# Recurrent scan: the triangular inversion on 32x32 diagonal blocks for its first four levels, joined to 64x64 in the fifth

## The chip, the cores and the metric

One Trainium2 chip, one of its cores. The metric is the device time of one execution, in microseconds. The kernel before takes 2808.89 us, the median of 3 runs (2808.25 to 2810.07).

## The reference, cut to what matters

The whole computation is two transformer blocks over 256 tokens (feed-forward layers, a differential attention, a recurrent mixer, memory and dilated attention). The change lies in the recurrent mixer alone, whose core is a scan over tokens, for each of 12 heads with a 64x64 state:

```python
def step(state, inp):
    r_t, w_t, k_t, v_t, kk_t, a_t = inp
    sa = jnp.einsum('bhvk,bhk->bhv', state, -kk_t)
    state = (state * w_t[:, :, None, :]
             + sa[..., None] * (kk_t * a_t)[:, :, None, :]
             + v_t[..., None] * k_t[:, :, None, :])
    return state, jnp.einsum('bhvk,bhk->bhv', state, r_t)
```

The term `sa` makes each token's update depend on the ones before it. Over a chunk of 64 tokens this is a system of equations with a unit lower triangular 64x64 matrix, so the scan can be done a chunk at a time once this matrix is inverted.

## The kernel before, in words

All of it runs on one core in float32. 97% of the span is TensorE work, most of it the products with the streamed weights (lines 2299 to 2301). The recurrent scan is a stretch of about 105 us without weight products, from 1909 to 2014 us of the span.

**Tiling of the scan.** The 12 heads are taken two at a time (RT = 6 iterations). A pair of heads has 4 chunks of 64 tokens for each head, so 8 triangular matrices of 64x64. They lie as 128 partitions (two chunks, rows `R[0]` and `R[1]`) by 4 units `m` of 64 columns. TensorE multiplies them as 64x64 tiles of its array, chunk 0 in rows and columns 0 to 63 and chunk 1 in 64 to 127. Each float32 matmul stands in the trace as two records.

**The inversion.** It grows the inverse `ti`, and its transpose `tit`, from blocks of 2 to 4, 8, 16, 32 and 64 in five levels. Level l of iteration i has four steps, each waiting for the one before:
- `level_p` (PE, L3017): P = L times `ti`, 8 matmuls into PSUM `INV[0]`
- `mask_p` (VectorE, L1982): the part of P that joins the blocks, into `pp`
- `level_t` (PE, L3030 and L3032): 8 matmuls for the growth of `ti` (not at level 4) and 8 for that of `tit`, into `INV[1]` and `INV[2]`
- `grow` (VectorE, L1988 and L1990): adds both to `ti` and `tit`

The matrices that it starts from come from `pairs_ti` (PE, L3000), `start_inverse` (VectorE, L1976 and L1978) and `start_transposed` (L1969 and L1970).

**The order.** It is written out by hand, for each engine, in a Python loop over i from 0 to 6. Between the steps of iteration i stand pieces of the neighbours: for i-1 the solution (`solve`, L3042), the read-out (`read_out`, L3055 to L3074), the state (`carry`, L3085) and the output (L3094); for i+1 the decay sums (L2939), the turn to token-major (L2968), the pairwise products (`pairs`, L2975), `pairs_ti` and `mix_values` (L3007). PE's order in a middle iteration is P0, solve, T0, decay sums, P1, read-out, T1, to tokens, P2, carry 0, pairs, T2, carry 1, pairs, P3, output, pairs, T3, pairs, P4, `pairs_ti`, T4, `mix_values`, where P and T are `level_p` and `level_t`. VectorE's queue has the same pieces in its own fixed order. ScalarE copies results out of PSUM (L1221 to L1242). Iteration 0 also carries the end of the weight splitting (L1315, 2.28 us each) and the bonus product (L2026) on VectorE.

Of the kernel before, what the change touches and what calls it, by code (L numbers as in the profile page):

```python
# [18 lines left out]
SHIFT = 8  # L19
# [8 lines left out]
CH = 64  # L28
# [25 lines left out]
def constants():  # L54

    p = np.arange(128)
    half = p // 64
    same = half[:, None] == half[None, :]
    parts = {}
    parts["ident"] = np.eye(128)  # L60
    parts["ones"] = np.ones((128, 128))
    parts["blk"] = same.astype(float)
    perm = np.zeros((128, 128))
    for f in range(128):
        perm[f ^ 16, f] = 1.0
# [24 lines left out]
    parts["lp_mask"] = np.concatenate([c_ < n_, c_ <= n_], 1).astype(float)  # L90
    def level(b, row, col):
        return ((row // (2 * b) == col // (2 * b)) & (row // b % 2 == 1) & (col // b % 2 == 0)).astype(float)
    parts["m1"], parts["m1t"] = level(1, c_, n_), level(1, n_, c_)
    for b in (2, 4, 8, 16, 32):
        parts[f"m{b}"] = level(b, c_, n_)


    parts["sel"] = np.zeros((128, 32))
    parts["sel"][p, 16 + half] = 1.0
    parts["sel8"] = np.zeros((128, 47))  # L100
    parts["sel8"][:, 39] = 1.0
    parts["spread"] = np.zeros((128, 8, 128))
    for i in range(8):
        parts["spread"][2 * i + half, i, p] = 1.0
        parts["spread"][32 + i, i] = 1.0
    parts["spread"] = parts["spread"].reshape(128, 1024)
    parts["ident64"] = np.concatenate([np.eye(64), np.eye(64)], 0)
# [167 lines left out]
def build(nc, W, ADA, AW, CB, XT, MEMT, VEC, CST, PM, BT, REL, LAM, W0B, LORA, GUP, OUT, stop=None):  # L275
# [13 lines left out]
    with ExitStack() as ctx:  # L289
# [154 lines left out]
              cst[:, cat["cos"]:cat["cos"] + 512].rearrange("p (m e n) -> p m e n", m=4, e=2)]  # L444
        xs = [cut(scr, 1024 + 1024 * j, 512, "p (m n) -> p m n", m=4) for j in range(2)]
        tx = cut(scr, 1536, 512, "p (m n) -> p m n", m=4)
        ti = cut(big, 7680 + SHIFT, 256, "p (m n) -> p m n", m=4)
        tit = [cut(hid, 0, 256, "p (m n) -> p m n", m=4), cut(scr, 8212, 256, "p (m n) -> p m n", m=4)]
        pp = cut(hid, 512, 256, "p (m n) -> p m n", m=4)
        ar = [cut(t, at, 512, "p (u e n) -> p u e n", u=2, e=2) for t, at in ((hid, 1024), (scr, 2560))]  # L450
        ends = cols[:, 24:36].rearrange("p (j c) -> p j c", j=3)

        VAR = [BANK[0], BANK[3]]
        MEAN = [BANK[i % 2][:, NX * (i // 2):NX * (i // 2 + 1)] for i in range(4)] + [BANK[2].rearrange("p (i n) -> p i n", n=NX)]
        Y_SQ = [lower[:, 8:10, :], lower[:, 10:12, :], hid[:, 1024:1536].rearrange("p (i n) -> p i n", n=NX)]
        INV = [ps_o[:, 0, 0:256], ps_o[:, 1, 0:256], ps_o[:, 1, 256:512]]
        FREE = [ps_o[:, 3, :], ps_g[:, 0, :], ps_u[:, 0, :], ps_u[:, 1, :], ps_g[:, 1, :]]
        be = cut(hid, 1536, 256, "p (u n) -> p u n", u=2)
        ka = cut(hid, 1792, 256, "p (u n) -> p u n", u=2)
# [841 lines left out]
        def _(dve):  # L1301
# [663 lines left out]

            def start_transposed(i):

                dve.wait_ge(rw["lpm"], 2 * i + 2)
                link(tt_(tit[i % 2], lp[i % 2][:, :, 0, :], over(C("m1t", CH), 4), mult))  # L1969
                tt_(tit[i % 2], tit[i % 2], over(C("ident64", CH), 4), add).then_inc(rw["tit"], 1)  # L1970

            def start_inverse(i):

                dve.wait_ge(rw["tib"], i + 1)
                for q, bank in enumerate((FREE[1], FREE[3])):
                    ins = tt_(ti[:, 2 * q:2 * q + 2, :], bank[:, 0:128].rearrange(by_unit, m=2), over(C("m1", CH), 2), mult)  # L1976
                link(ins)
                tt_(ti, ti, over(C("ident64", CH), 4), add).then_inc(rw["lmask"], 1)  # L1978

            def mask_p(i, l):  # L1980
                dve.wait_ge(rw["p"], 5 * i + l + 1)
                tt_(pp, INV[0].rearrange(by_unit, m=4), over(C(f"m{2 << l}", CH), 4), mult).then_inc(rw["pm"], 1)  # L1982

            def grow(i, l):

                dve.wait_ge(rw["t"], 5 * i + l + 1)
                if l < 4:
                    tt_(ti, ti, INV[1].rearrange(by_unit, m=4), add).then_inc(rw["ti"], 1)  # L1988
                t = tit[i % 2]
                tt_(t, t, INV[2].rearrange(by_unit, m=4), add).then_inc(rw["tt"], 1)  # L1990

            def readout(i):
                dve.wait_ge(rw["rp"], i + 1)
# [73 lines left out]
                pairs(0, q, "lp", lp, FREE[q], "lpm")  # L2067
            for q, b in enumerate((4, 0)):
                pairs(0, q, "mp", mp, FREE[b], "mpm")
            start_transposed(0)  # L2070
            start_inverse(0)
            for i in range(RT + 1):
                inv, post, pre = i < RT, i > 0, i + 1 < RT
                if inv:
# [209 lines left out]
        def _(pe):  # L2284
# [659 lines left out]
            for t in range(2, len(A_IN)):  # L2944
# [12 lines left out]
            R = [slice(0, 64), slice(64, 128)]  # L2957
            def tok(i, e, m):
                return tmaj[i % 2][:, e, m % 2, 64 * (m // 2):64 * (m // 2) + 64]

# [31 lines left out]
            def pairs_ti(i):  # L2992
                pe.wait_ge(rw["lpm"], 2 * i + 2)
                if i >= 2:
                    pe.wait_ge(rw["ss2"], 2 * (i - 1))
                for q in range(2):
                    for u in range(2):
                        for c in range(2):
                            t = slice(CH * c, CH * (c + 1))
                            ins = mm(FREE[1 + 2 * q][R[c], CH * u:CH * (u + 1)], ar[i % 2][R[q], u, 0, t], be[R[q], u, t], start=True, stop=True)  # L3000
                ins.then_inc(rw["tib"], 1)

            def mix_values(i):
# [6 lines left out]
            def level_p(i, l):  # L3010
                if l:
                    pe.wait_ge(rw["ti"], 4 * i + l)
                else:
                    pe.wait_ge(rw["lmask"], i + 1)
                for m in range(4):
                    for c in range(2):
                        ins = mm(INV[0][R[c], CH * m:CH * (m + 1)], lp[i % 2][R[c], m, 0, :], ti[R[c], m, :], start=True, stop=True)  # L3017
                ins.then_inc(rw["p"], 1)

            def level_t(i, l):  # L3020
                pe.wait_ge(rw["pm"], 5 * i + l + 1)
# [2 lines left out]
                else:  # L3024
                    pe.wait_ge(rw["tit"], i + 1)
                for m in range(4):
                    t = slice(CH * m, CH * (m + 1))
                    if l < 4:
                        for c in range(2):
                            mm(INV[1][R[c], t], tit[i % 2][R[c], m, :], pp[R[c], m, :], start=True, stop=True)  # L3030
                    for c in range(2):
                        ins = mm(INV[2][R[c], t], pp[R[c], m, :], tit[i % 2][R[c], m, :], start=True, stop=True)  # L3032
                ins.then_inc(rw["t"], 1)

            def solve(i):
# [224 lines left out]
```

## Time and profile before

| | |
|---|---|
| time, median of 3 | 2808.89 us |
| time of the profiled execution | 2802.01 us |
| its span | 2800.3 us |
| PE busy | 2706.9 us, 97% |
| VectorE (DVE) busy | 2045.4 us, 73% |
| ScalarE (ACT) busy | 1012.2 us, 36% |
| mean granted TensorE clock | 0.984 |

PE's busy time counts a matmul from its start to its modelled end, so it includes the latency after the last column. A stretch in which PE is called busy can still be one in which it waits for columns of a result. How fast PE really goes is read from the starts of successive groups.

### The profile page before, as it was taken

The page shows a single profiled execution, that of the slowest core. Times are in us where ns is not written, and L with a number is a line of the kernel's source. Part 1 is how long each engine was busy: PE and PEld are TensorE (multiplying, and loading weights), DVE is VectorE, ACT ScalarE, POOL GpSimd, SP SyncE. Part 2 cuts the span into 40 slices and gives each one's busy share as a digit, 9 for nine tenths or more (in the row PEclk, how much of TensorE's full clock was granted, in tenths as well). Part 3 has the DMA queues.
Part 4 walks back from the last instruction along what each step waited for, and adds up shares of the span by engine and source line. Part 5 has one row for each costly group of instructions (what it writes and reads, how often), then busy time and mean ns, then how long its engine had stood idle before and what let it go on. Part 6 is the DMA issues. An engine that isn't in the chain of part 4 may idle for free.

```text
span 2800.3 us, 48988 instructions
## 1 busy us (share of the span) xinstructions
PE 2706.9 (97%) x19262; PEld 2409.6 (86%) x19262; DVE 2045.4 (73%) x3070; ACT 1012.2 (36%) x1169; POOL 145.8 (5%) x206
## 2 busy tenths in 40 slices
PE   6999999999999999999999899998999999998999
PEld 4888878888888888888799899977799989996999
DVE  5888887777787766766677776766777776665777
ACT  4222234222242222333343533552144444353433
POOL 1000011000010000100010000000000010000000
PEclk9999999999999999999999999999999999998999
DMA  9455532444424443222154344521044554443354
GB/s 363 165 189 180 179 133 103 152 150 150 168 111 154 158 153 141 97 106 90 72 188 187 135 180 181 199 82 57 3 171 180 195 143 180 180 180 68 121 191 184
DMA packets 68706, 421.44 MB, mean 150 GB/s; under 512 B 7672, under 2 KB 8824, under 8 KB 26592
## 3 DMA queue, kind: packets, MB, share of 16 engines
q1 hardware_dynamic: 48176, 343.36, 32.7%
q0 software_dynamic: 20432, 76.69, 8.5%
q8 instruction: 71, 1.16, 0.2%
q14 instruction: 27, 0.22, 0.0%
HBM read 418.95 MB, written 1.07 MB: 150 GB/s over the span
## 4 chain that ended last, share of the span: by engine, by line
PE 89%; DVE 7%; ACT 2%; issue 1%; DMA 1%; SPq 0%; ACTq 0%; DVEq 0%
PE ps_o L2299 11%; PE ps_o L2300 10%; PE ps_o L2301 10%; PE ps_g L2299 8%; PE ps_u L2299 8%; PE ps_u L2300 8%; PE ps_u L2301 8%; PE ps_g L2300 8%; PE ps_g L2301 8%; DVE wlo L1315 2%; PE ps_o L2543 1%; DMA scr<-in_AW 1%; DVE tsq L1368 1%; PE ps_g L2520 1%; PE ps_o L2529 1%
## 5 line engine op out<-in xcount | busy, mean ns | idle before, releaser
L787 ACT ACTIVATE whi<-wraw 128x2048 fp32r<-128x2048 f32 x314 | 598.9, 1911 | 783.3 <-PE ps_u L2301 346.0
L1315 DVE TENSOR_TENSOR wlo<-wraw,whi 128x2048 fp32r<-128x2048 f32 x314 | 711.5, 2287 | 123.8 <-ACT whi L787 123.3
L2299 PE MATMUL ps_g<-hh,wlo 128*128 128x256 f32 (+1 forms) x1464 | 464.7, 317 | 9.5 <-ACT tsq L903 7.0
L2301 PE MATMUL ps_g<-hh,whi 128*128 128x256 f32 (+1 forms) x1464 | 463.1, 316 | 0.0
L2300 PE MATMUL ps_g<-hl,whi 128*128 128x256 f32 (+1 forms) x1464 | 462.7, 316 | 0.0
L2299 PE MATMUL ps_u<-hh,wlo 128*128 128x256 f32 (+1 forms) x1464 | 461.9, 315 | 0.0
L2301 PE MATMUL ps_u<-hh,whi 128*128 128x256 f32 (+1 forms) x1464 | 461.8, 315 | 0.0
L2300 PE MATMUL ps_u<-hl,whi 128*128 128x256 f32 (+1 forms) x1464 | 461.4, 315 | 0.0
L2299 PE MATMUL ps_o<-ah,wlo 128*128 128x256 f32 (+1 forms) x1360 | 433.3, 319 | 3.5 <-DVE x L1421 3.5
L2301 PE MATMUL ps_o<-ah,whi 128*128 128x256 f32 (+1 forms) x1360 | 432.5, 318 | 0.0
L2300 PE MATMUL ps_o<-al,whi 128*128 128x256 f32 (+1 forms) x1360 | 432.0, 318 | 0.0
L1421 DVE SCALAR_TENSOR_TENSOR x<-ps_o,gcol,x 128x256 f32<-128x256 f32 x640 | 281.4, 479 | 119.4 <-PE ps_o L2301 113.4
L2299 PEld LDWEIGHTS ps_g<-hh,wlo 128*128 128x128 f32 x1464 | 276.8, 189 | 32.5 <-issue 13.6
L2300 PEld LDWEIGHTS ps_g<-hl,whi 128*128 128x128 f32 x1464 | 276.9, 189 | 18.7
L2301 PEld LDWEIGHTS ps_g<-hh,whi 128*128 128x128 f32 x1464 | 276.7, 189 | 18.8
L2299 PEld LDWEIGHTS ps_u<-hh,wlo 128*128 128x128 f32 x1464 | 275.5, 188 | 18.8 <-issue 0.2
L2301 PEld LDWEIGHTS ps_u<-hh,whi 128*128 128x128 f32 x1464 | 275.4, 188 | 18.8
L2300 PEld LDWEIGHTS ps_u<-hl,whi 128*128 128x128 f32 x1464 | 275.4, 188 | 18.7
L2299 PEld LDWEIGHTS ps_o<-ah,wlo 128*128 128x128 f32 x1360 | 255.5, 188 | 24.0 <-DVE wlo L1315 3.0
L2300 PEld LDWEIGHTS ps_o<-al,whi 128*128 128x128 f32 x1360 | 255.5, 188 | 18.7
L2301 PEld LDWEIGHTS ps_o<-ah,whi 128*128 128x128 f32 x1360 | 255.5, 188 | 18.7
L907 ACT ACTIVATE ah<-tsq 128x512 fp32r<-128x512 f32 (+1 forms) x85 | 66.7, 784 | 427.0 <-PE ps_o L2301 413.7
(494 smaller groups left out, 3750.5 us busy)
## 6 DMA issues: line engine op xcount, KB each, us to landing
wraw<-in_W SPq DMA_DIRECT2D x315, 1024.0 KB, 4.9
scr<-in_ADA POOLq DMA_DIRECT2D x126, 512.0 KB, 4.4
scr<-in_AW SPq DMA_DIRECT2D x5, 1024.0 KB, 26.5
big<-in_AW SPq DMA_DIRECT2D x4, 1024.0 KB, 14.0
scr<-bias_rows POOLq DMA_DIRECT2D x8, 384.0 KB, 9.2
x<-in_XT SPq DMA_DIRECT2D x1, 2048.0 KB, 9.0
x<-in_MEMT POOLq DMA_DIRECT2D x2, 1024.0 KB, 7.0
cst<-in_CST POOLq DMA_DIRECT2D x1, 1511.5 KB, 6.6
```

The costliest lines, as they stand in the source:

```text
L787: nc.scalar.activation(whi[:, n % SLOTS, :], wraw[:, n % SLOTS, :], ACT.Copy).then_inc(w_hi, 1)
L907: nc.scalar.activation(dst[:, :, 0:N], tmp[:, :, 0:N], ACT.Copy).then_inc(a_hi, 1)
L1315: tt_(wlo[:, n % SLOTS, :], wraw[:, n % SLOTS, :], whi[:, n % SLOTS, :].bitcast(f32), sub).then_inc(w_lo, 1)
L1368: stt(dst, src(d)[:, HALVES[j]], A(d, j), rstd[:, HALVES[j]], mult, mult).then_inc(nm_t, 1)
L1421: ins = stt(x[:, d, HALVES[j]], src[:, HALVES[j]], gate(d, j), x[:, d, HALVES[j]], mult, add)
L2299: mm(out, a[1], b[0], start=first, stop=False)
L2300: mm(out, a[0], b[1], start=False, stop=False)
L2301: return mm(out, a[0], b[0], start=False, stop=last)
L2520: ins = mm(bank[rows, b, c], q, k, start=True, stop=True)
L2529: ins = nc.tensor.transpose(att_flip(g, b), probs[g % 2][:, b * 128:(b + 1) * 128], ident)
L2543: ins = mm(att_out(g)[unit["rows"]], unit["v"][b], probs_t[a][g % 2][:, b, :], start=b == 0, stop=b == nb - 1)
```

## The change

- `pairs_ti` computes only the 32x32 diagonal blocks of the starting matrices, and their transposes as well: 32 matmuls with 64 rows and 32 columns of the array in place of 8 of 64x64. `start_transposed` takes the transposes from there, not from the masked `lp`.
- For levels 0 to 3 `ti`, the new `ti_t`, `pp` and `INV` hold 4 units of 32 columns on 128 partitions. `level_p` has 16 matmuls of 32x32 at the four diagonal tiles of the array in place of 8; `level_t` has 32 in place of 16. VectorE's operations on them have 128 elements per partition in place of 256.
- Level 4 joins two 32x32 blocks to one 64x64 transpose in PSUM (`WHOLE`): its `level_p` has 8 matmuls of the block below the diagonal (P), 8 that turn the upper block and 8 that turn the lower one (these with 64 columns and zeros), its `level_t` 8 matmuls. `mask_p` is a copy, `grow` one copy of 256 elements into `tit`.
- `start_inverse` of the next iteration stays where it is on VectorE, `start_transposed` too, but for the first iteration their order is exchanged. The masks in the constants become 32 columns wide (224 columns less in all).

```diff
-            def start_inverse(i):
-
                 dve.wait_ge(rw["tib"], i + 1)
                 for q, bank in enumerate((FREE[1], FREE[3])):
-                    ins = tt_(ti[:, 2 * q:2 * q + 2, :], bank[:, 0:128].rearrange(by_unit, m=2), over(C("m1", CH), 2), mult)
+                    ins = tt_(ti_t[:, 2 * q:2 * q + 2, :], bank[:, 64:128].rearrange(by_unit, m=2), over(C("m1t", 32), 2), mult)
                 link(ins)
-                tt_(ti, ti, over(C("ident64", CH), 4), add).then_inc(rw["lmask"], 1)
+                tt_(ti_t, ti_t, over(C("ident32", 32), 4), add).then_inc(rw["tit"], 1)
...
             def mask_p(i, l):
                 dve.wait_ge(rw["p"], 5 * i + l + 1)
-                tt_(pp, INV[0].rearrange(by_unit, m=4), over(C(f"m{2 << l}", CH), 4), mult).then_inc(rw["pm"], 1)
+                if l < 4:
+                    tt_(pp, INV[0].rearrange(by_unit, m=4), over(C(f"m{2 << l}", 32), 4), mult).then_inc(rw["pm"], 1)
+                else:
+                    nc.vector.tensor_copy(pp, INV[0].rearrange(by_unit, m=4)).then_inc(rw["pm"], 1)
 
             def grow(i, l):
 
                 dve.wait_ge(rw["t"], 5 * i + l + 1)
                 if l < 4:
                     tt_(ti, ti, INV[1].rearrange(by_unit, m=4), add).then_inc(rw["ti"], 1)
-                t = tit[i % 2]
-                tt_(t, t, INV[2].rearrange(by_unit, m=4), add).then_inc(rw["tt"], 1)
+                    tt_(ti_t, ti_t, INV[2].rearrange(by_unit, m=4), add).then_inc(rw["tt"], 1)
+                else:
+                    nc.vector.tensor_copy(tit[i % 2], WHOLE.rearrange(by_unit, m=4)).then_inc(rw["tt"], 1)
...
-                for q in range(2):
-                    for u in range(2):
-                        for c in range(2):
-                            t = slice(CH * c, CH * (c + 1))
-                            ins = mm(FREE[1 + 2 * q][R[c], CH * u:CH * (u + 1)], ar[i % 2][R[q], u, 0, t], be[R[q], u, t], start=True, stop=True)
+                for u in range(2):
+                    for t in range(4):
+                        for q in range(2):
+                            a, b = ar[i % 2][R[q], u, 0, Q[t]], be[R[q], u, Q[t]]
+                            mm(FREE[1 + 2 * q][Q[t], 32 * u:32 * (u + 1)], a, b, start=True, stop=True)
+                            ins = mm(FREE[1 + 2 * q][Q[t], 64 + 32 * u:96 + 32 * u], b, a, start=True, stop=True)
...
+                if l == 4:
+                    for m in range(4):
+                        for c in range(2):
+                            mm(WHOLE[Q[2 * c], CH * m:CH * m + 32], ti[Q[2 * c], m, :], ident64[Q[2 * c], 0:32], start=True, stop=True)
                 for m in range(4):
-                    for c in range(2):
-                        ins = mm(INV[0][R[c], CH * m:CH * (m + 1)], lp[i % 2][R[c], m, 0, :], ti[R[c], m, :], start=True, stop=True)
+                    o = slice(32 * m, 32 * (m + 1))
+                    if l < 4:
+                        for t in range(4):
+                            ins = mm(INV[0][Q[t], o], lp[i % 2][Q[t], m, 0, HALF[t % 2]], ti[Q[t], m, :], start=True, stop=True)
+                    else:
+                        for c in range(2):
+                            ins = mm(INV[0][Q[2 * c + 1], o], lp[i % 2][Q[2 * c], m, 0, HALF[1]], ti[Q[2 * c], m, :], start=True, stop=True)
                 ins.then_inc(rw["p"], 1)
+                if l == 4:
+                    for m in range(4):
+                        for c in range(2):
+                            mm(WHOLE[Q[2 * c + 1], CH * m:CH * (m + 1)], ti[Q[2 * c + 1], m, :], ident64[Q[2 * c + 1], :], start=True, stop=True)
...
                 for m in range(4):
-                    t = slice(CH * m, CH * (m + 1))
+                    o = slice(32 * m, 32 * (m + 1))
                     if l < 4:
+                        for t in range(4):
+                            mm(INV[1][Q[t], o], ti_t[Q[t], m, :], pp[Q[t], m, :], start=True, stop=True)
+                        for t in range(4):
+                            ins = mm(INV[2][Q[t], o], pp[Q[t], m, :], ti_t[Q[t], m, :], start=True, stop=True)
+                    else:
                         for c in range(2):
-                            mm(INV[1][R[c], t], tit[i % 2][R[c], m, :], pp[R[c], m, :], start=True, stop=True)
-                    for c in range(2):
-                        ins = mm(INV[2][R[c], t], pp[R[c], m, :], tit[i % 2][R[c], m, :], start=True, stop=True)
+                            h = Q[2 * c + 1]
+                            ins = mm(WHOLE[Q[2 * c], CH * m + 32:CH * (m + 1)], pp[h, m, :], ti_t[h, m, :], start=True, stop=True)
                 ins.then_inc(rw["t"], 1)
```

## Rows read from the trace of the kernel before

**Rows 1.** Stages view, iterations 0 and 2; busy time and records of each engine

```profile
core 0: us, PE busy (x) PEld busy (x) DVE busy (x) ACT busy (x) POOL busy (x), PEclk, DMA share, GB/s
1909.40:1929.80 20.40, 14.24 (x299) 12.15 (x300) 14.79 (x29) 2.08 (x6) 0.00 (x0) 0.92 0.27 104
...
1946.20:1962.60 16.40, 15.59 (x416) 13.74 (x416) 12.09 (x40) 3.03 (x8) 0.00 (x0) 1.00 0.01 3
```

**Rows 2.** Timeline of PE, iteration 2: start, length, line, shape, records, idle before

```profile
1946.15 0.68 PE L3017 MATMUL ps_o<-big,tsq 64*64 64x64 f32 x16
1946.66 1.04 PE L3042 MATMUL ps_o<-scr 64*64 64x128 f32 x16
1947.61 0.33 PE L3030 MATMUL ps_o<-hid 64*64 64x64 f32 x4
...
1948.36 0.28 PE L3030 MATMUL ps_o<-hid 64*64 64x64 f32 x4
1948.47 0.28 PE L3032 MATMUL ps_o<-hid 64*64 64x64 f32 x4
1948.69 0.70 PE L2939 MATMUL ps_g<-cst,big 128*128 128x256 f32 x2
...
1954.90 0.27 PE L3085 MATMUL ps_u<-scr 64*64 64x64 f32 x2 [0.29 <-DVE scr L2006]
...
1962.61 0.68 PE L3017 MATMUL ps_o<-big,x 64*64 64x64 f32 x16
```

**Rows 3.** Timeline of PE, iteration 5: 64x64 tiles to the whole array and back

```profile
2001.55 0.28 PE L3032 MATMUL ps_o<-scr,hid 64*64 64x64 f32 x4
2001.76 0.70 PE L3102 MATMUL ps_g<-tsq,cst 128*128 128x256 f32 x2
2002.39 0.68 PE L3017 MATMUL ps_o<-big,x 64*64 64x64 f32 x16
...
2010.07 1.04 PE L3108 MATMUL ps_g<-big,cst 128*16 128x256 f32 x4
2011.03 0.68 PE L3032 MATMUL ps_o<-scr,hid 64*64 64x64 f32 x16
```

**Rows 4.** Timeline of PE: two stretches that use four 64x64 tiles at once

```profile
1905.84 0.69 PE L2975 MATMUL ps_g<-hid 64*64 64x128 f32 x16 [0.71 <-ACT scr L1234]
1906.33 0.60 PE L2975 MATMUL ps_o<-hid 64*64 64x128 f32 x8
...
1950.61 0.22 PE L3064 MATMUL ps_u<-cst,x 64*64 64x64 f32 x2
1950.62 0.27 PE L3062 MATMUL ps_u<-x,scr 64*64 64x64 f32 x3
1950.67 0.23 PE L3064 MATMUL ps_u<-cst,x 64*64 64x64 f32 x3
1950.73 0.22 PE L3062 MATMUL ps_u<-x,scr 64*64 64x64 f32 x2
1950.73 0.27 PE L3064 MATMUL ps_u<-cst,x 64*64 64x64 f32 x3
1950.79 0.23 PE L3062 MATMUL ps_u<-x,scr 64*64 64x64 f32 x3
```

**Rows 5.** Timeline of VectorE, iteration 2

```profile
1953.92 0.34 DVE L2004 TENSOR_TENSOR scr<-ps_u,cst 128x64 f32<-128x64 f32 x2
...
1961.29 0.41 DVE L1964 TENSOR_TENSOR cst<-ps_o,cst 128x256 f32<-128x256 f32 x1
1961.62 0.28 DVE L1976 TENSOR_TENSOR big<-ps_g,cst 128x128 f32<-128x128 f32 x1
1961.82 0.28 DVE L1976 TENSOR_TENSOR big<-ps_u,cst 128x128 f32<-128x128 f32 x1
```

**Rows 6.** Timeline of PE, iteration 0: end of T1, and what it waits for next

```profile
1914.84 0.28 PE L3032 MATMUL ps_o<-hid 64*64 64x64 f32 x4
1917.05 0.44 PE L2968 MATMUL ps_g<-cst,scr 128*128 128x128 f32 x2 [1.93 <-DVE hid L1937]
```

More of the change, by code:

```diff
@@ L92, in level @@
         return ((row // (2 * b) == col // (2 * b)) & (row // b % 2 == 1) & (col // b % 2 == 0)).astype(float)
-    parts["m1"], parts["m1t"] = level(1, c_, n_), level(1, n_, c_)
-    for b in (2, 4, 8, 16, 32):
-        parts[f"m{b}"] = level(b, c_, n_)
+    c32_, n32_ = s_ % 32, np.arange(32)[None, :]
+    parts["m1"], parts["m1t"] = level(1, c32_, n32_), level(1, n32_, c32_)
+    for b in (2, 4, 8, 16):
+        parts[f"m{b}"] = level(b, c32_, n32_)
+    parts["ident32"] = (c32_ == n32_).astype(float)
     parts["sel"] = np.zeros((128, 32))
@@ L446, in build @@
         tx = cut(scr, 1536, 512, "p (m n) -> p m n", m=4)
-        ti = cut(big, 7680 + SHIFT, 256, "p (m n) -> p m n", m=4)
+        ti = cut(big, 7680 + SHIFT, 128, "p (m n) -> p m n", m=4)
+        ti_t = cut(big, 7808 + SHIFT, 128, "p (m n) -> p m n", m=4)
         tit = [cut(hid, 0, 256, "p (m n) -> p m n", m=4), cut(scr, 8212, 256, "p (m n) -> p m n", m=4)]
-        pp = cut(hid, 512, 256, "p (m n) -> p m n", m=4)
+        pp = cut(hid, 512, 128, "p (m n) -> p m n", m=4)
         ar = [cut(t, at, 512, "p (u e n) -> p u e n", u=2, e=2) for t, at in ((hid, 1024), (scr, 2560))]
@@ L455, in build @@
         Y_SQ = [lower[:, 8:10, :], lower[:, 10:12, :], hid[:, 1024:1536].rearrange("p (i n) -> p i n", n=NX)]
-        INV = [ps_o[:, 0, 0:256], ps_o[:, 1, 0:256], ps_o[:, 1, 256:512]]
+        INV = [ps_o[:, 0, 0:128], ps_o[:, 1, 0:128], ps_o[:, 1, 128:256]]
+        WHOLE = ps_o[:, 2, 256:512]
         FREE = [ps_o[:, 3, :], ps_g[:, 0, :], ps_u[:, 0, :], ps_u[:, 1, :], ps_g[:, 1, :]]
@@ L1966, in start_transposed @@
             def start_transposed(i):
-                dve.wait_ge(rw["lpm"], 2 * i + 2)
-                link(tt_(tit[i % 2], lp[i % 2][:, :, 0, :], over(C("m1t", CH), 4), mult))
-                tt_(tit[i % 2], tit[i % 2], over(C("ident64", CH), 4), add).then_inc(rw["tit"], 1)
+                dve.wait_ge(rw["tib"], i + 1)
+                for q, bank in enumerate((FREE[1], FREE[3])):
+                    ins = tt_(ti_t[:, 2 * q:2 * q + 2, :], bank[:, 64:128].rearrange(by_unit, m=2), over(C("m1t", 32), 2), mult)
+                link(ins)
+                tt_(ti_t, ti_t, over(C("ident32", 32), 4), add).then_inc(rw["tit"], 1)
             def start_inverse(i):
@@ L1975, in start_inverse @@
                 for q, bank in enumerate((FREE[1], FREE[3])):
-                    ins = tt_(ti[:, 2 * q:2 * q + 2, :], bank[:, 0:128].rearrange(by_unit, m=2), over(C("m1", CH), 2), mult)
+                    ins = tt_(ti[:, 2 * q:2 * q + 2, :], bank[:, 0:64].rearrange(by_unit, m=2), over(C("m1", 32), 2), mult)
                 link(ins)
-                tt_(ti, ti, over(C("ident64", CH), 4), add).then_inc(rw["lmask"], 1)
+                tt_(ti, ti, over(C("ident32", 32), 4), add).then_inc(rw["lmask"], 1)
             def mask_p(i, l):
                 dve.wait_ge(rw["p"], 5 * i + l + 1)
-                tt_(pp, INV[0].rearrange(by_unit, m=4), over(C(f"m{2 << l}", CH), 4), mult).then_inc(rw["pm"], 1)
+                if l < 4:
+                    tt_(pp, INV[0].rearrange(by_unit, m=4), over(C(f"m{2 << l}", 32), 4), mult).then_inc(rw["pm"], 1)
+                else:
+                    nc.vector.tensor_copy(pp, INV[0].rearrange(by_unit, m=4)).then_inc(rw["pm"], 1)
             def grow(i, l):
@@ L2069, in _ @@
                 pairs(0, q, "mp", mp, FREE[b], "mpm")
+            start_inverse(0)
             start_transposed(0)
-            start_inverse(0)
             for i in range(RT + 1):
@@ L2957, in _ @@
             R = [slice(0, 64), slice(64, 128)]
+            Q = [slice(32 * j, 32 * j + 32) for j in range(4)]
+            HALF = [slice(0, 32), slice(32, 64)]
+            ident64 = C("ident64", CH)
             def tok(i, e, m):
```

## The prediction

> **What bounds the kernel now.** The page comes first: TensorE is busy for 97% of the span, and nearly all of the chain that ended last is the weight products, which the change doesn't touch. Only the scan can change, some 105 of 2800 us. I read its stages by the stages view [rows 1]: in a middle iteration PE is "busy" for 15.59 of 16.40 us, VectorE for 12.09 with 40 operations. So both are near to full, and the busy share can't say which one ends last. For that I read PE's timeline of iteration 2 [rows 2], and in it not the lengths but the starts. From the first P0 (1946.15) to the next (1962.61) it takes **16.46 us**.
>
> How fast does PE go through the 64x64 tiles? Four records start at 1948.36 and the next four at 1948.47 [rows 2]: 29 ns a record, 58 ns a matmul. A group then shows some 0.2 us more than it occupies (16 records: 0.46 us, shown as 0.68), since the last matmul takes its time to come out. With 128 columns the same engine needs 55 ns a record (L3042, 16 records, 1.04 less 0.16 us). So time per record follows the columns: 26 ns for 64 columns more, and about 4 ns of overhead per record and tile, hardly any issue cost.
>
> The iteration, put together from this: P five times 0.464, T four times 0.93 and once 0.46, together 6.5 us; `pairs_ti` 0.42; other work 6.9 (48 records of 128 columns at 55 ns, 2.6; decay sums and transposes 12 records at the whole array, 1.7, since a record of 256 columns, which goes over them twice, has 512 columns at 2.4 GHz, the level granted here (1.00 in rows 1), so 0.21 us; the 80 of the read-out, which run at between 14 [rows 4] and 29 ns, at 20, 1.6; 36 others at 29 ns, 1.0). That leaves 2.6 us of 16.46, which are waits for VectorE and something that happens at the whole-array groups.
>
> **What a change of the tile size costs.** T's last four records start at 2001.55, so the next record could start at 2001.67; the 128x128 group starts at 2001.76, 0.09 late. Its two records occupy 0.43, and the next 64x64 group starts 0.63 after it, 0.20 late [rows 3]. The other direction and shape: four records of 128x16 occupy 0.85 us, and T4 starts 0.96 after them, 0.11 late [rows 3]. So each change of the tiling costs 0.09 to 0.20 us, mean 0.14. Before, an iteration has four of them (0.6 us), which leaves 2.0 us of waits for VectorE such as the 0.29 at L3085 [rows 2].
>
> The Trainium skill (TensorEngine Tiling (Array Packing), Tiling Modes) has the rule that speaks against this change: changing the mode, not the tile, drains the engine. It gives no price. The rows agree that there is one.
>
> **The change, part by part, in a middle iteration.**
> 1. *Levels 0 to 3, PE.* Twice as many matmuls with half the columns: P 32 records, T 64. A 32-column record has 27 ns of columns and 4 ns of overhead, 31 ns on its tile; with four tiles in parallel that is 7.8 ns a record. No row shows 32x32 tiles. Nearest are stretches with four 64x64 tiles: 16 records of 128 columns in 0.49 us (31 ns, ideal 27.5), and 13 records of 64 columns from 1950.61 to 1950.79 (14 ns, ideal 14.5) [rows 4]. So four tiles do run together and a record can be issued every 14 ns; whether faster is not shown, as these were limited by columns. Bounds: 7.8 and 14.5 ns. I take **10**, near the lower one because every row scales with columns and none shows an issue limit, and above it because 14 ns was the best stretch of a read-out that I put at 20. P becomes 0.32 (was 0.46), T 0.64 (was 0.93): 5.58 becomes 3.84, **-1.7 us** (bounds -2.6 and 0).
> 2. *Level 4.* P4 has 16+16 records of 32 columns on two tiles (0.25+0.25), then 16 of 64 columns (0.46), T4 16 records (0.25): 1.21 in place of 0.93, **+0.3**. The 0.46 stand behind P's signal and beside VectorE's copy, so they prolong PE, not that wait.
> 3. *`pairs_ti`.* 64 records at 10 ns, 0.64 in place of 0.42, **+0.2** (bounds +0.1 and +0.5).
> 4. *Changes of the tiling.* Now every neighbour of a P or T is one, and `pairs_ti` stands in a third mode (64x32) between P4 and T4: 20 in an iteration in place of 4. The 16 new ones are between 64- and 32-row tiles, which no row shows. Above are the 0.20 of rows 3, below nothing, if they were free as 64x64 tiles among each other are. I take 0.12: between the 0.09 and the mean 0.14, since a drain through 32 rows should be no longer than one of the whole array. **+1.9 us** (bounds 0 and +3.2).
> 5. *VectorE.* 256 elements occupy 0.33 us (1961.29 to 1961.62), 128 elements 0.20 (1961.62 to 1961.82), 64 elements 0.13 to 0.17 [rows 5]. Masks and growths of levels 0 to 3: 12 operations 0.13 shorter; the mask of level 4 too; the two starts 0.5 less together. About 2.1 us less VectorE work in an iteration. Alone it is worth only as much as PE waits for it: 2.0 us of waits.
> 6. *What then is late next.* The waits before P0, T0, P3, P4 and T4 are short (0.05 to 0.4 us); with operations 0.13 shorter, latencies shorter, and PE held up by the drains and the added groups, they are covered. What stays is that before carry 0, behind VectorE's unchanged chain of L2001 to L2006: 0.4. **-1.6 us.**
>
> PE's sum: 3.84+1.21+0.64+6.9+0.6+1.9+0.4 = 15.5 in place of 16.46: **-1.0 us** an iteration, five times -5. Iteration 0 is different: PE is busy 14.24 of 20.40 us [rows 1] and VectorE sets the pace, as when PE stands for 1.93 us until L1937 [rows 6]. There some ten shorter steps count in full (0.13 each, and PE's groups of P and T 0.15 and 0.3 shorter where nothing stands between): -2.4, against +0.9 for changes of tiling on that path: -1.5. The two exchanged starts of the first iteration, the smaller constants (115 KB of some 420 MB) and the tail iteration 6 I cost at nothing; the constants land while PE still waits for its first weights. Sum **-6.5 us**. For the profiled execution (2802.01, span 2800.3) that gives 2795.5; for the median of runs, 6.9 above it, 2808.9 becomes **2802.4**.
>
> **The rivals.**
> *A, records are issued at 14.5 ns or tiles don't run four at a time, and a change costs 0.145 or more (ends slower).* Four diagonal tiles share one PSUM bank, and the rows with four tiles at once had two banks; two at a time give 15.5 ns. Levels then stay at 5.57, `pairs_ti` 0.93, all 20 changes 2.9, level 4 1.21, others 6.9, waits 0.2: 17.7, +1.2 an iteration, iteration 0 even: +6, 2815; at 0.20 a change +10, 2819. It decides from the point at which 0.448 x (ns a record) + 16 x (us a change) is over 7.3: at 10 ns from 0.18 us a change, at 0.12 us from 12 ns.
> *B, full parallelism and cheap changes.* 7.8 ns and 0.05 us: PE's sum is 13.6 with waits that come back (VectorE's chain of mask, growth and the neighbours' pieces holds it at some 13.5 to 14): -2.7 an iteration, -2.5 in iteration 0: 2793.
> *C, PE starts no record sooner than 25 ns after another.* In this kernel it would make P 0.8 and T 1.6 us, `pairs_ti` 1.6: +5 an iteration and more, some +30 in all, 2839. The best stretch of rows 4 with 14 ns speaks against it. The Trainium skill (TensorE: Matmul & The Clock Gate, Part 1) states such a floor of about 25 ns, however few the columns; by that rule this case would decide, the trace disagrees for different tiles.
> *D, the change does little.* The gain of PE's levels goes into drains and VectorE's shorter work stays hidden, because waits move and don't vanish: -0.2 an iteration, 2808.
>
> **How the numbers follow.** Forecast 0.45 (its own range 2798 to 2807), A 0.23, B 0.14, C 0.04, D 0.14. The range for 8 in 10 leaves out C and part of A and B: 2793 to 2818. A measurement of this kernel tells 0.2%, 5.6 us, from no change. Faster by more than this: B and some seven tenths of the forecast's case, 0.46. Within it: the rest of that, D and the milder part of A, 0.32. Slower: most of A, and C, 0.22.
>
> **What would show it.** Right: T in 0.6 to 0.7 us from start to next start, starts of records on four tiles within 31 ns, a gap of about 0.1 us between each P or T and its 64x64 neighbours, waits on L1982 and L1988 nearly gone, an iteration of 15.5 us. Wrong: T at 0.9 or more (A), at 1.6 (C), gaps of 0.2 (A) or none (B), waits for L1988 as long as now (D).

## The result and the profile after

The changed kernel takes **2827.24 us** (median of 4 runs, 2823.4 to 2830.25) where the kernel before takes 2809.32 (4 runs, 2808.25 to 2810.07): a ratio of 1.0067, 95% interval 1.005 to 1.0084. It is 17.9 us slower. The forecast was 2802.4, the range ended at 2818.

The page of the changed kernel, with busy time, share and instructions of each engine, and its row for the instruction queue:

```profile
span 2821.7 us, 52258 instructions
PE 2727.9 (97%) x20894; PEld 2423.3 (86%) x20894; DVE 2035.5 (72%) x3076; ACT 1012.3 (36%) x1169; POOL 145.9 (5%) x206
q8 instruction: 84, 1.38, 0.2%
```

The page of before has `PE 2706.9 (97%) x19262` and `q8 instruction: 71, 1.16, 0.2%`. So TensorE got 1632 more records, and as many weight loads, and the queue that fetches instructions carried 13 packets more, of 16 KB each (1.38 MB by 84). The same holds for all fourteen traces here: from the fewest records (e6: 18686, 66 packets) to the most (e3: 22526, 96) it is 128 added records a packet, and the others lie within one packet of that line. VectorE has 10 us less to do, as intended.

Where the time is lost shows in the stages view, cut from one start of `start_inverse` to the next (columns: us, PE busy, PEld, DVE, ACT, POOL, granted clock, DMA share, GB/s). These rows answer to rows 1. First iterations 0 and 2 of before, cut in the same way, then 0 to 4 of after:

```profile
1908.34:1928.52 20.18, 12.99 (x274) 10.88 (x274) 14.48 (x29) 2.47 (x7) 0.00 (x0) 0.94 0.26 103
1945.16:1961.62 16.46, 15.64 (x422) 13.79 (x420) 12.15 (x40) 3.06 (x8) 0.00 (x0) 1.00 0.01 3
```

```profile
1908.37:1927.94 19.57, 15.08 (x560) 12.05 (x562) 13.14 (x31) 2.47 (x7) 0.00 (x0) 0.73 0.30 111
1927.94:1948.85 20.91, 18.40 (x694) 15.37 (x696) 10.43 (x41) 3.07 (x8) 0.00 (x0) 0.83 0.02 4
1948.85:1968.22 19.37, 17.90 (x694) 15.00 (x694) 10.41 (x40) 3.07 (x8) 0.00 (x0) 0.84 0.02 4
1968.22:1988.76 20.54, 18.51 (x694) 15.33 (x695) 10.49 (x41) 3.07 (x8) 0.00 (x0) 0.83 0.02 5
1988.76:2009.01 20.25, 17.93 (x694) 15.02 (x694) 10.51 (x41) 3.07 (x8) 0.00 (x0) 0.83 0.02 4
```

Iteration 0 is 0.6 us shorter. A middle iteration takes 20.3 us (mean of the four) in place of 16.46. Up to the scan's start the two traces agree to 0.03 us; the first weight product behind the scan starts at 2026.93 before (so the stretch without weight products ends there, not at 2014) and at 2043.33 after, so **the scan costs 16.4 us more**, which is nearly the difference of the medians. (The profiled spans differ by 21.4. The other 5 us lie outside the change, and are less than executions of the kernel before differ by: 2802.77 to 2812.0 in the 20 runs beside e1.)

Two things in these rows are new: 694 records in place of 422, and a granted clock of 0.83 in place of 1.00. What PE does in the middle of an iteration is in its timeline (start, busy, tile shape, count, and in brackets the idle time before and what ended it):

```profile
1955.38 0.45 PE L3036 MATMUL ps_o<-big,tsq 32*32 32x32 f32 x32
1955.77 0.47 PE L3085 MATMUL ps_o<-x,scr 64*64 64x64 f32 x16
...
1957.59 0.26 PE L3056 MATMUL ps_o<-hid,big 32*32 32x32 f32 x8
1957.68 0.24 PE L3058 MATMUL ps_o<-big,hid 32*32 32x32 f32 x8
1957.74 0.24 PE L3056 MATMUL ps_o<-hid,big 32*32 32x32 f32 x8
1957.80 0.24 PE L3058 MATMUL ps_o<-big,hid 32*32 32x32 f32 x8
```

Groups of 8 records start 0.06 to 0.09 us apart: **8 to 9 ns a record** (all 64 of this T start within 0.56 us), with all four diagonal tiles at work. P of 32 records occupies 0.26 us and its 64x64 neighbour (L3085) starts 0.39 after it, 0.13 late. The levels themselves do what they were meant to. But elsewhere the same code stands still in the middle of a group:

```profile
1943.68 0.19 PE L3058 MATMUL ps_o<-big,hid 32*32 32x32 f32 x1
1944.69 0.22 PE L3058 MATMUL ps_o<-big,hid 32*32 32x32 f32 x3 [0.82 <-issue]
...
1947.00 0.19 PE L3013 MATMUL ps_u<-hid 64*32 64x32 f32 x1
1948.32 0.21 PE L3013 MATMUL ps_g<-hid 64*32 64x32 f32 x1 [1.13 <-issue]
```

Nothing that the profile knows of was missing ("issue"), and the two halves of these groups wait for no semaphore. Between the restarts at 1944.69 and 1948.32 lie 3.63 us and **127 records**. The pair at 1963.56 and 1967.11 has 128 records in 3.55 us, the pair at 1986.40 and 1989.88 has 127 in 3.48, and restarts further apart lie 254, 508 or 635 records from each other, a multiple of 127. That is one packet of the instruction queue (some records are missing from a trace). So PE seems to have used up its instructions and to go on when the next packet is there: 27 to 29 ns a record, however short the records.

The times of the packets bear this out. These two lines are of the view of DMA for 1941.50 to 1950.90, in 40 slices of 0.235 us:

```profile
GB/s 0 0 70 0 0 0 0 0 0 0 0 0 0 0 0 0 0 0 70 0 0 35 0 0 0 0 0 0 0 0 0 0 0 0 70 0 0 0 0 0
q8 instruction: 3, 0.05, 2.5%
```

The three slices of 70 GB/s are the starts of the three packets: 1942.08, 1945.80 and 1949.54 (the 35 is another queue). The first ends at 1943.45, and PE restarts 1.24 us later, at 1944.69; the second ends at 1946.97, and PE restarts 1.34 us later. It is so at all 13 restarts of the scan behind a wait of over 0.3 us: the last packet ended 1.2 to 1.6 us before, and in 12 of them the next starts 1.1 to 1.4 us behind the restart. With 0.9 to 1.4 us for the packet itself a round takes 3.3 us or more, and brings 128 records. The same 1.2 to 1.6 us stand before all the restarts of this size in e3, e5 and e7, and before all but one in e11. The trace of before has its packets mostly 3.7 us and more apart, and no such wait.

The waits of PE in iterations 1 to 4, before and after (us in total, times, longest):

```profile
PE ps_u L3085 <- DVE scr L2006: 1.2, 4, 0.3
PE ps_o L3032 <- DVE hid L1982: 1.1, 4, 0.3
PE ps_o L3017 <- DVE big L1988: 0.5, 3, 0.2
```

```profile
PE ps_g L3013 <- issue: 2.1, 2, 1.1
PE ps_o L3058 <- issue: 1.3, 3, 0.8
PE ps_u L3115 <- DVE scr L2015: 1.0, 4, 0.4
PE ps_o L3062 <- issue: 0.9, 1, 0.9
PE ps_o L3044 <- issue: 0.7, 1, 0.7
```

The waits for VectorE's masks and growths are gone, as forecast; the one for carry 0 (L2006, now L2015) stays. In their place stand waits for instructions, 7.0 us in these four iterations with the four shorter rows left out here, 1.75 an iteration. VectorE now waits for PE: `DVE big L1996 <- PE ps_o L3058` 25.4 us in 18 times over the scan, where L1988 waited 16.9 for L3032.

Finer windows of after show the clock (the last column but two):

```profile
1941.00:1944.60 3.60, 2.87 (x127) 2.33 (x127) 1.64 (x6) 0.00 (x0) 0.00 (x0) 1.00 0.02 5
1944.60:1948.30 3.70, 2.50 (x127) 2.08 (x128) 1.70 (x6) 0.00 (x0) 0.00 (x0) 0.97 0.02 7
1948.30:1950.30 2.00, 1.98 (x46) 1.75 (x45) 1.39 (x7) 0.00 (x0) 0.00 (x0) 0.50 0.04 8
1950.30:1953.80 3.50, 3.50 (x114) 3.03 (x112) 0.83 (x3) 0.98 (x2) 0.00 (x0) 0.50 0.00 0
```

PE is busy for 5.4 of 7.3 us, and then runs at 1.2 GHz, the lower of its two levels, from 1948.3 on for more than 5.5 us; there `solve` shows 1.97 us (L3072, 16 records of 128 columns) where it showed 1.04. The next two half-speed stretches, from 1968.5 and from 1989.0, begin behind the restart at 1967.11 and in the wait that ends at 1989.88.

### The profile page after: what moved, and what is told of

It reads as the page before. It is cut to its first block, busy times and chain, and to the rows that moved or that the text cites. A ratio compares the mean times of both kernels' runs of the same rounds, so it can differ in the third digit from the quotient of the medians.

```text
span 2821.7 us, 52258 instructions
## 1 busy us (share of the span) xinstructions
PE 2727.9 (97%) x20894; PEld 2423.3 (86%) x20894; DVE 2035.5 (72%) x3076; ACT 1012.3 (36%) x1169; POOL 145.9 (5%) x206
## 3 DMA queue, kind: packets, MB, share of 16 engines
q8 instruction: 84, 1.38, 0.2%
## 4 chain that ended last, share of the span: by engine, by line
PE 89%; DVE 7%; ACT 2%; issue 1%; DMA 1%; SPq 0%; ACTq 0%; DVEq 0%
PE ps_o L2308 11%; PE ps_o L2309 10%; PE ps_o L2310 10%; PE ps_g L2308 8%; PE ps_u L2308 8%; PE ps_u L2309 8%; PE ps_u L2310 8%; PE ps_g L2309 8%; PE ps_g L2310 8%; DVE wlo L1318 1%; PE ps_o L2552 1%; DMA scr<-in_AW 1%; DVE tsq L1371 1%; PE ps_o L2538 1%; PE ps_u L2529 1%
```

## The experiments

The question was which of three things costs the 4 us an iteration: the supply of instructions (**S**), the changes of tiling (**M**), or the clock (**K**). In all edits `small(n)` issues n tiny float32 matmuls in 32x32 tiling, each of 32 rows and 4 columns of data, so 2n records, whose result goes to an unused part of PSUM. (The array's columns that each uses are 4 in e1 to e5 and 32 in e11.) What was expected before each run names it as S, M and K too.

**Changes of tiling alone (e1), and more records alone (e2, e3, e5)**, in the kernel before, whose tiles stay 64x64:

```diff
+            def small(n):
+                one_, two_ = C("ident64", 4), C("ident64", 4)
+                for j in range(n):
+                    z = slice(32 * (j % 4), 32 * (j % 4) + 32)
+                    mm(ps_o[:, 0, 256:260][32 * (j % 4):32 * (j % 4) + 4], one_[z], two_[z], start=True, stop=True)
...
+                if l < 4:
+                    small(1)    # e1; 17 in e2, 34 in e5, 68 in e3
```

> The kernel before, with one extra 32x32 matmul of 4 columns (2 records) behind each T of levels 0 to 3: 8 more changes of the tiling in an iteration, hardly more instructions (424 records in place of 416). Theory M (the time went into changes of the tiling): 8 x 0.12 to 0.20 us an iteration, less what waits cover, so +0.5 to +1.5 us an iteration and +3 to +8 us in all. Theory S (PE's instructions arrive in blocks of 128 records, one in at least 3.6 us, 28 ns a record on average): 424 records ask for 11.9 us, nothing is starved, no idle PE without a wait. Theory K (the granted clock falls with small tiles): no fall here, the work is still 64x64.

> The same with 17 small matmuls in each of the four places: 136 records more, 552 in an iteration. S: 552 x 28 ns = 15.5 us, still under the iteration's own length of 16.4 us and more, so at most single short gaps; the iteration grows only by what the small ones occupy (34 records at 8 ns, 0.27 us a place, 1.1 us) and the 8 changes of the tiling: 17.5 to 18.5 us, +6 to +12 us in all. M: the same changes as in the run with one small matmul, so the same time plus 1.1 us an iteration.

> The kernel before with 34 small matmuls behind each T of levels 0 to 3: 272 records more, 688 in a middle iteration, exactly as many as the changed kernel has, but with the levels in 64x64 tiles and 8 changes of the tiling more in place of 16. S (supply of instructions): 688 x 28 ns = 19.3 us an iteration, gaps without a wait after every 128 records, +15 to +22 us in all, as in the changed kernel. Columns and changes of the tiling alone, continued from 17 small ones (17.0 us an iteration with 136 records more): 18.0 us, +8 to +11 us in all, no gaps.

> The same with 68 small matmuls in each place: 544 records more, 960 in an iteration, more than the 688 of the changed kernel. S: 960 x 28 ns = 26.9 us an iteration, +10 us each and +50 to +60 us in all, with PE idle for no wait every 125 to 128 records although the levels are as before. M and the columns alone: 4 x 136 records at 8 ns = 4.4 us and 1 us of changes: 21.5 us an iteration, +25 to +30 us in all, no such gaps.

| small(n) | records an iteration | ratio to before (95%) | iterations 1 to 4, us |
|---|---|---|---|
| 1 | 424 | 1.0005 (0.9994 to 1.0016) | 16.59, 16.59, 16.58, 16.59 |
| 17 | 552 | 1.0026 (1.0015 to 1.0038) | 17.48, 17.15, 16.99, 16.98 |
| 34 | 688 | 1.0098 (1.0077 to 1.0118) | 20.08, 22.71, 21.49, 19.70 |
| 68 | 960 | 1.0275 (1.0245 to 1.0305) | 27.74, 31.16, 28.98, 29.68 |

e1 has 8 changes of tiling more in an iteration and takes 0.13 us longer: M falls. e2 adds 0.5 us to its later iterations. From 552 to 688 records, by tiny matmuls again, it jumps by 4 us more; e5 has just the 688 records of the changed kernel and loses 26.2 us (2834.61 against 2808.44), more than the change itself and than the 15 to 22 that S had put down (5 of them in iteration 0). Two of its stages and two restarts in its timeline:

```profile
1958.87:1981.58 22.71, 18.95 (x692) 16.75 (x690) 12.51 (x41) 3.06 (x8) 0.00 (x0) 0.97 0.01 4
2003.07:2022.77 19.70, 18.09 (x691) 16.10 (x687) 12.41 (x40) 3.06 (x8) 0.00 (x0) 1.00 0.02 5
```

```profile
1976.29 0.38 PE L2975 MATMUL ps_g<-scr,hid 64*64 64x128 f32 x3 [0.81 <-issue]
...
1980.39 0.37 PE L3017 MATMUL ps_o<-big,tsq 64*64 64x64 f32 x1 [1.19 <-issue]
```

Here the 64x64 levels are untouched, and the clock is at 0.97 and 1.00 (0.90 and 0.87 in iterations 1 and 3), so neither K nor the small tiles of the levels can be the cause: with the clock at 1.00 the last of these iterations still takes 19.70 us. Part of it is the time that the added records themselves take, some 2 us by 272 records at 7.7 ns (68 of them start within 0.52 us). Per record: 21.0 us by 688 is 30.5 ns (e5), 29.4 by 960 is 30.6 (e3), 20.3 by 688 is 29.5 (the changed kernel). Up to 552 records an added one cost about 4 ns, from there on 30. e3 lost more than S had put down, 78 us, of which 12 lie in iteration 0 (32.11 us).

**Fewer records (e4, e6)**: only units 0 and 1 of four in the matmuls of levels 0 to 3, in the changed kernel (e4) and in the one before (e6). Both leave out the growth of units 2 and 3, so they are no kernels to use, only clocks for the time.

```diff
-                for m in range(4):
+                for m in range(2 if l < 4 else 4):
```

> The changed kernel with only units 0 and 1 of 4 in the matmuls of levels 0 to 3 (the growth of the others is left out): 192 records fewer, 496 in an iteration; all changes of the tiling stay, all tiles stay 32x32. S: 496 x 28 ns = 13.9 us, so no more gaps every 128 records, an iteration of 14 to 15 us, 10 us and more below the kernel before. M: 20 changes of the tiling still cost, 18 us or more an iteration. K (small tiles lower the granted clock whatever the supply): the clock still falls in each iteration, 17 us or more.

> The kernel before with only units 0 and 1 of 4 in the matmuls of levels 0 to 3 (the growth of the others is left out): the counterpart to the same cut of the changed kernel. 96 records fewer, 320 in an iteration, no supply limit (9 us). PE loses 4 x (0.23 + 0.46) = 2.8 us of columns, and VectorE's full-width operations become the bound (they are on the path of every level): 14.5 to 15.5 us an iteration, -6 to -10 us in all. If the changed kernel with the same cut (14.9 us an iteration) is not faster than this, small tiles gain nothing even where they aren't starved.

e4: ratio 0.9975 (0.9959 to 0.9991); e6: 0.9964 (0.9952 to 0.9975). Their iterations:

```profile
1928.20:1944.32 16.12, 14.94 (x504) 12.50 (x506) 10.25 (x40) 3.06 (x8) 0.00 (x0) 0.89 0.02 6
1944.32:1958.94 14.62, 13.39 (x502) 11.09 (x500) 10.16 (x41) 3.06 (x8) 0.00 (x0) 1.00 0.02 4
```

```profile
1945.58:1960.23 14.65, 13.13 (x326) 11.09 (x324) 12.03 (x40) 3.06 (x8) 0.00 (x0) 1.00 0.01 3
```

With 496 records the changed kernel needs 14.4 to 16.1 us, 5 us less for 192 records less, which S explains. But I had expected the gaps to vanish and 10 us to be gained on the kernel before; gaps of 0.4 to 0.8 us stayed, and it was 7 us: 496 records in 14.6 us are 29.5 ns a record, the same limit. And e6, with 64x64 tiles, is as fast (14.65 us, 11 us below): at half the work the small tiles gain nothing.

**The changed kernel without the surplus records (e7)**: VectorE makes the transpose of `ti`, so T has 32 records less at each level and `pairs_ti` 32 less; nothing is left out. 528 records an iteration.

```diff
-                    tt_(ti_t, ti_t, INV[2].rearrange(by_unit, m=4), add).then_inc(rw["tt"], 1)
+                    dve.wait_ge(rw["ti"], 4 * i + l + 1)
+                    nc.vector.transpose(ti_t_flat, ti_flat).then_inc(rw["tt"], 1)
...
                         for t in range(4):
                             mm(INV[1][Q[t], o], ti_t[Q[t], m, :], pp[Q[t], m, :], start=True, stop=True)
-                        for t in range(4):
-                            ins = mm(INV[2][Q[t], o], pp[Q[t], m, :], ti_t[Q[t], m, :], start=True, stop=True)
```

> The changed kernel, but the transpose of the inverse at levels 0 to 3 is made by VectorE from the grown inverse (32x32 blocks, 128 elements, in place of an addition of the same size), and at the start too: PE loses 16 matmuls a level and 16 in pairs_ti, 160 records, 528 in an iteration, with nothing of the work left out. S: 528 x 28 ns = 14.8 us, at most small gaps, the granted clock stays up, 14.5 to 15.5 us an iteration, -6 to -12 us against the kernel before. M (20 changes of the tiling remain as in the changed kernel): 17 us or more an iteration, slower than before. K (small tiles lower the clock): slower than before.

Measured 2806.53 against 2808.44, ratio 0.9997 (0.9987 to 1.0007): the change's 17.9 us are gone, but nothing of the 6 to 12 us that S promised is gained on the kernel before. The iterations take 16.55, 16.20, 17.47 and 15.41 us, not the 14.5 to 15.5 that I expected. The supply still binds, in the dense parts:

```profile
1987.43 0.26 PE L3036 MATMUL ps_o<-big,tsq 32*32 32x32 f32 x7 [0.61 <-issue]
...
1991.37 0.32 PE L3056 MATMUL ps_o<-hid,big 32*32 32x32 f32 x15 [0.34 <-issue]
...
1995.10 0.33 PE L3020 MATMUL ps_g<-x,cst 64*64 64x64 f32 x2 [0.97 <-issue]
```

**Fewer still (e8, e10)**: `pairs_ti` goes, VectorE takes the starting matrices from the masked `lp`, level 4 keeps 8+8 matmuls and VectorE puts the blocks together. 464 records. e8 has the start's operations in one block ahead of `mask_p` of level 4; e10 is the same with them a step earlier.

```diff
+                link(tt_(start_w, lp[i % 2][:, :, 0, :], over(C("m1t", CH), 4), mult))
+                tt_(start_t, start_w[:, :, 0:32], start_w[:, :, 32:64], add)
...
+                nc.vector.transpose(ti_flat, start_flat).then_inc(rw["lmask"], 1)
...
+                ts_(tit[i % 2][:, :, 0:32], ti_t, C("even", 1), None, mult)
+                ts_(tit[i % 2][:, :, 32:64], ti_t, C("odd", 1), None, mult).then_inc(rw["tib"], 1)
```

> The run with the transpose on VectorE, with three more pieces taken off PE and nothing left out: pairs_ti is gone (the start comes from the masked pairs, transposed by VectorE), level 4 has 8 matmuls for P and 8 for T and no matmuls that only turn blocks (VectorE puts the blocks into place). 64 records fewer, 464 in a middle iteration, 18 changes of the tiling, all levels still in 32x32 tiles; VectorE has some 0.9 us more. S: 464 x 30 ns = 13.9 us, no regular gaps, the clock at full from iteration 1 on, 14 to 15 us an iteration, -8 to -14 us against the kernel before. M and K (changes of the tiling, small tiles and their clock): no better than the run with the transpose on VectorE, 16.4 us an iteration and no gain.

> The kernel with 464 records an iteration had no supply gaps but a wait of 1.77 us in each iteration on the copy L1996 (mask of level 4), which stood on VectorE behind the three operations of the next start; its clock fell by this idle stretch (granted clock 0.87 to 0.90). Here these operations stand two places earlier, where VectorE was idle, and the copy goes first. Nothing else changes, PE's work and its changes of the tiling are the same. S: the wait goes, 14.2 to 14.9 us an iteration (13.9 us is the supply's floor at 30 ns), clock 1.00 from iteration 2 on, -7 to -12 us against the kernel before. M and K: no gain, since no tile and no change of the tiling is gone.

e8 took 2808.13 against 2808.23, ratio 1.0 (0.9989 to 1.0012), where 8 to 14 us less were expected. The regular gaps were gone, and a wait of my own making had come: `1963.81 0.38 PE L3058 MATMUL ps_o<-big,hid 32*32 32x32 f32 x13 [1.77 <-DVE hid L1996]`, the mask of level 4 queued behind the start. **e10 took 2801.26 against 2807.57, ratio 0.9969 (0.996 to 0.9979): it beats both kernels**, by 6 us where 7 to 12 were expected. (One of its ten executions took 15024.86 us. It doesn't enter the ratio, and hardly moves the median.) Two of its iterations:

```profile
1944.66:1960.33 15.67, 14.15 (x464) 11.35 (x464) 11.00 (x43) 3.07 (x8) 0.00 (x0) 0.89 0.01 3
1977.07:1992.49 15.42, 13.97 (x464) 11.61 (x464) 10.99 (x42) 3.06 (x8) 0.00 (x0) 0.89 0.01 4
```

Its iterations also miss what I expected of them, 14.2 to 14.9 us: the clock is at 0.80 to 0.89 in each iteration, though PE's longest wait in iterations 1 to 4 is 0.7 us, and it stands still for instructions once, for 0.4 us.

**More records on small tiles (e11)**: e10 with `small(37)` behind T of levels 0 to 2, which brings it back to 686 records, now with the same tiling on both sides. (The like of it was planned for e8, as e9, and gave no time.)

```diff
+                if l < 3:
+                    small(37)
```

> The same kernel with 37 matmuls of 32x32 with 4 columns behind T of levels 0 to 2: 222 records more, 686 in an iteration as in the changed kernel (688), with no change of the tiling more. S: 686 x 30 ns = 20.6 us an iteration, gaps for no wait after 128 records and a lower clock, +15 to +25 us against the kernel before. Columns alone: 3 x 74 records at 8 ns, 1.8 us an iteration on the run without them, 16 to 17 us, about even with the kernel before.

2840.15 against 2807.57, ratio 1.0115 (1.0097 to 1.0132), iterations of 22.8 to 24.3 us at a clock of 0.65 to 0.71, and restarts such as `1948.02 0.23 PE L3065 MATMUL ps_o<-hid,big 32*32 32x32 f32 x3 [0.89 <-issue]`, 127 records behind the one at 1944.09. The dose brings the gaps back where e10 has one: S again, this time with no change of tiling added. But 686 records in 23.4 us are 34 ns each, above the limit, and the loss of 33 us is above the 15 to 25 that S had put down; between the waits PE ran at half speed for over half of the time. So here the clock costs time as well, and the two shares aren't told apart.

**Does standing still lower the clock? (e12, e13)** The kernel before, its tiles and records untouched, with the mask written again to make PE wait: four times at levels 1 and 4 (e12), twice at all five (e13).

```diff
+                for _ in range(4 if l in (1, 4) else 0):    # e13: range(2)
+                    link(tt_(pp, INV[0].rearrange(by_unit, m=4), over(C(f"m{2 << l}", CH), 4), mult))
```

> The kernel before with the mask of levels 1 and 4 written four times more (the same values), each write waiting for the last, some 0.42 us each: PE's records and tiles are those of before (416 an iteration), it only stands still for some 1.7 us twice in an iteration. This asks whether idle stretches alone make the granted clock fall. Theory K1 (the clock falls because PE stands still): iterations of 16.5 + 3 to 3.4 = 19.5 to 19.9 us from the waits, and on top the clock at about 0.8 to 0.9, another 1 to 3 us, 20.5 to 23; in all +20 to +35 us. Theory K2 (idle stretches of this size alone don't do it, thin 32x32 records do): 19.5 to 19.9 us at a granted clock of 1.00 in iterations 1 to 4, +16 to +20 us in all. I take K1 at 0.5.

> The same with two more writes at each of the five levels: five stretches of some 0.84 us in place of two of 1.7, with nearly the same sum (up to 4.2 us, less where PE's other groups hide some). K1 with the length of a single idle stretch mattering: clock nearer to 1.00 than in the kernel with two long ones. K1 with the sum mattering: the same clock as there. K2: 1.00 in iterations 1 to 4 and 19 to 20.5 us an iteration.

```profile
1980.35:2001.32 20.97, 17.07 (x422) 15.37 (x422) 15.70 (x49) 3.06 (x8) 0.00 (x0) 0.93 0.01 4
```

```profile
1980.84:2001.39 20.55, 16.40 (x422) 14.01 (x420) 16.26 (x50) 3.07 (x8) 0.00 (x0) 1.00 0.02 4
```

The first row is e12 (iterations 22.05, 21.18, 20.97, 19.95 us; clock 0.88, 0.91, 0.93, 0.99; ratio 1.0098, 1.0069 to 1.0127), the second e13 (21.27, 20.56, 20.55, 20.56; clock 0.92, then 1.00 three times; ratio 1.0084, 1.0049 to 1.0119). So long stretches alone do lower the clock of 64x64 work: in e12 PE waits up to 2.1 us at a time. Stretches of up to 1.2 us don't, in the last three of these iterations, though e13 stands still for 4.2 us in each iteration (20.55 less 16.40), twice as much as the changed kernel (2.3 in the row of iteration 4). (In e13's iteration 0, with waits of up to 2.1 us, the clock was 0.59, yet before has waits of 2.1 and 1.9 us in its own and got 0.94; the length of a wait alone doesn't decide.) K1, in which standing still is all that matters, falls for stretches of the changed kernel's size, and so does K2, by which it never matters. What remains is that 32x32 work holds the clock less well than 64x64 work with the same pauses: e10 pauses for 0.7 us at most and falls to 0.80 to 0.89, e13 pauses longer and more and keeps 1.00; of the two kernels with half the units, e6 (64x64) kept 1.00 in all four iterations and e4 (32x32) in two, with waits of up to 0.5 and 0.6 us. Why, no run tells, and e4 and e7, which kept 1.00 in two of four iterations each, show that it isn't a matter of the tile size alone.

## Why the prediction was wrong

1. *Levels 0 to 3 on PE* ("none shows an issue limit", 10 ns): the rate inside a group was even 8 to 9 ns, near the lower bound. **The sentence on the issue limit is the step that failed.** It was right for a group and wrong for an iteration. I counted the time of every record and never the records: 688 in place of 416 (rows 1), so that with 15.5 us the forecast asked for 22.5 ns a record, sustained, while the best that this kernel showed was 16.46 us by 416, 40 ns. What the sum left out is that PE's instructions come in packets of 128 records, one in some 3.6 us. e5 shows that 688 records cost that much with the old tiles as well, and e2 that 552 are nearly free. 688 times 28 to 30 ns is 19.3 to 20.6 us, which is the iteration as measured.
2. *Rival C*, 0.04, had the size nearly right (2839 forecast, 2827 measured) for a reason that fell, so by luck: PE does start records 8 ns apart. The Trainium skill (TensorE: Matmul & The Clock Gate, Part 1) states a start-to-start floor of about 25 ns; inside a group the trace disagrees again, now for 32x32 tiles. From one restart to the next, 127 records and more, the average is 27 to 29 ns, over whole iterations 28 to 31. I had dismissed the rival by the best stretch of rows 4, 13 records long; a stretch so short can't show a limit that sets in from one packet of 128 records to the next.
3. *Changes of the tiling*, +1.9: probably mis-sized, and not the cause. The timeline shows 0.13 at a single one (P1 to carry), as forecast; but e1 pays 0.13 us in all for eight of them with four small matmuls. Sixteen are so worth between 0.3 and 2.1 us an iteration, which the forecast already held. The rival that rested on them (A) needed 0.18 each at 10 ns a record; neither came.
4. *Waits*, -1.6 out of 2.0: the waits for L1982 and L1988 did vanish, as the list of waits shows. But they were smaller than I took them for: 1.6 us in four iterations before, beside 1.2 for carry 0, so 0.7 an iteration (counted from the modelled end of the last matmul, up to 0.2 us after PE could have gone on). My 2.6 us was the remainder of a sum, not a row; the view of the waits would have corrected it.
5. *The clock*, which I took as 1.00 as in rows 1: 0.83. What it costs here is estimated, not shown. With 688 records the supply alone fills the 20 us (e5, at 0.87 to 1.00, is slower still), so most of the half-speed stretches probably lie where PE would have waited for instructions instead. The packets allow an estimate: of the 18 intervals between 1942.08 and 2009.41, 15 are 3.4 to 3.8 us, the supply's own pace, and the other three exceed 3.6 by 2.4 us in all, so that some 0.7 us an iteration are left for the clock and everything else. In e10, where the supply hardly binds, half-speed stretches probably are what keeps 15.8 us from the 14.2 to 14.9 expected; no run has e10 at 1.00.
6. *VectorE*, -2.1 us an iteration: near in size (12.15 to 10.43 busy, -1.7) and worth nothing, as it no longer ends last.
7. *Iteration 0*, -1.5: -0.6 measured (20.18 to 19.57). The sign was right, VectorE sets its pace; PE ran it at a clock of 0.73 instead of 0.94.
8. *Level 4 and `pairs_ti`*, +0.5 together: their time was small, but they are 80 of the 272 added records (`pairs_ti` 48, level 4 32), and e8 and e10 gain by dropping them.

Of the range: its upper end came from A. The trace of before has no row for the limit of supply, only that 416 records in 16.46 us (40 ns each) were had. The missing term had bounds of nothing and 688 x 40 ns = 27.5 us an iteration, and the range should have reached well above 2818 for it.

## What to carry to other kernels

Before cutting matmuls into smaller tiles, count instructions as well as columns: records by time, over a stretch of several hundred records, against the densest such stretch that the kernel already runs. The only version here that gained by small tiles is the one in which the number of instructions hardly grew, e10 (464 records in place of 416), where another engine took over what had doubled the matmuls. And idle time that the trace puts down to "issue" in the middle of a group, at even distances in records, is the sign of an engine that waits for its own program; the times of the packets of the instruction queue then confirm it.

## What the runs showed of the hardware

- TensorE used up instructions faster than they came. It stood still, mostly for 0.3 to 1.6 us, and in the densest stretches of five kernels (after, e3, e5, e7, e11) every 127 or 128 records; the sustained rate was 28 to 31 ns a record (matmul and weight load), with 64x64 tiles (e5, e3) as with 32x32 (after).
- An instruction packet of 16 KB brought 128 records (18686 records with 66 packets, 22526 with 96). It took 0.9 to 1.4 us, a waiting TensorE restarted 1.2 to 1.6 us behind its end, and in after the packets started 3.4 us apart at the least.
- In the kernel before, with its 16.5 us an iteration, the cost set in between 552 and 688 records; in shorter iterations single waits came sooner (528 records in 16.4 us in e7, 496 in 15.1 in e4).
- Four diagonal 32x32 tiles took a record every 8 to 9 ns, writing different partitions of one PSUM bank: 64 records started within 0.56 us.
- Eight more changes between 64x64 and 32x32 tiling cost 0.13 us an iteration in all.
- The granted clock stayed at 1.00 through pauses of up to 1.2 us in 64x64 work (e13), fell to 0.88 to 0.99 with pauses of 2.1 (e12), and fell to 0.80 to 0.89 with pauses of 0.7 at most in 32x32 work (e10).
- VectorE's transpose of 128 elements a partition in 32x32 blocks took 0.31 us (`L1998 DVE STREAM_TRANSPOSE big<-big 128x128 f32<-128x128 f32 x16 | 5.0, 311` in e7's groups), no less than the 0.29 of an operation on two inputs of that size (L1988).
